# Turning the FFN's middle blocks in 32x32 pieces on VectorE and ScalarE instead of transposing them on TensorE

## The reference, cut to what matters

```python
def swiglu(h, wi, wo):
    g, u = jnp.split(h @ wi, 2, axis=-1)
    return (jax.nn.silu(g) * u) @ wo

def ffn_sublayer(x, shift, scale, gate, norm_w, wi, wo):
    return x + 0.5 * gate * swiglu(modulate(rms_norm(x, norm_w), shift, scale), wi, wo)
```

## Time and profile before

| | |
|---|---|
| time, median of 3 runs | 2223.12 us (2222.61 to 2223.47) |
| the profiled execution, from first to last instruction | 2220.9 us |
| TensorE busy | 2187.9 us, 99%, 10448 instructions |
| VectorE busy | 1634.8 us, 74% |
| ScalarE busy | 936.0 us, 42% |
| GpSimd busy | 64.5 us, 3% |
| share of the DMA queues, main one | 55.9% |

### The profile page before, as it was taken

The page is one execution under the profiler, slowest core; times in us unless marked ns, Lnnn a source line. Parts: engine busy times, 40 slices in busy tenths (PEclk is TensorE's granted clock), DMA queues, the critical chain, the costliest instruction groups (busy, mean ns, idle before and its releaser), DMA issues.

```text
span 2220.9 us, 28326 instructions
## 1 busy us (share of the span) xinstructions
PE 2187.9 (99%) x10448; PEld 1752.6 (79%) x10448; DVE 1634.8 (74%) x1881; ACT 936.0 (42%) x1098; POOL 64.5 (3%) x55
## 2 busy tenths in 40 slices
PE   6999999999999999999999999999999999999999
PEld 3568777777777778888888888888888888888887
DVE  3447888888888889756767888984577676776856
ACT  3333333333333346455554344464443444344443
POOL 0001000000000000001500000100000000000000
PEclk9999999999999999999999999999999999999999
DMA  9999888788888876555536776846665757567573
GB/s 364 387 369 307 286 315 314 270 293 290 306 301 283 281 262 222 198 171 170 186 114 228 269 254 233 278 159 207 228 227 190 264 189 264 189 195 259 188 228 132
DMA packets 273332, 548.13 MB, mean 247 GB/s; under 512 B 9014, under 2 KB 9418, under 8 KB 273008
## 3 DMA queue, kind: packets, MB, share of 16 engines
q1 hardware_dynamic: 212676, 423.69, 55.9%
q10 hardware_dynamic: 57484, 113.47, 14.2%
q0 software_dynamic: 3104, 10.05, 1.6%
HBM read 543.71 MB, written 3.46 MB: 246 GB/s over the span
## 4 chain that ended last, share of the span: by engine, by line
PE 94%; DVE 3%; DMA 1%; issue 1%; ACT 1%; SPq 0%; DVEq 0%; ACTq 0%
PE ps L697 29%; PE ps L699 29%; PE ps L698 29%; PE ps L638 1%; PE ps L623 1%; DMA ada_w_sb<-in_ada_w 1%; PE ps L774 1%; DVE w_lo L1789 1%; DVE acc L2003 0%; PE ps L1091 0%; PE ps L684 0%; PE ps L1159 0%; PE ps L1167 0%; DVE xm L1909 0%; ACT w_hi L1338 0%
## 5 line engine op out<-in xcount | busy, mean ns | idle before, releaser
L1338 ACT CAST w_hi<-raw_w 128x1024 fp32r<-128x1024 f32 x728 | 764.8, 1053 | 1162.2 <-PE ps L699 1114.1
L1789 DVE TENSOR_TENSOR w_lo<-raw_w,w_hi 128x1024 fp32r<-128x1024 f32 x728 | 896.5, 1235 | 405.3 <-ACT w_hi L1338 402.2
L697 PE MATMUL ps<-w_hi,xT_hi 128*128 128x512 f32 x2080 | 821.8, 395 | 5.6 <-DVE xT_lo L1877 4.2
L699 PE MATMUL ps<-w_hi,xT_lo 128*128 128x512 f32 x2080 | 811.1, 390 | 0.0
L698 PE MATMUL ps<-w_lo,xT_hi 128*128 128x512 f32 x2080 | 810.8, 390 | 0.0
L697 PEld LDWEIGHTS ps<-w_hi,xT_hi 128*128 128x128 f32 x2080 | 391.0, 188 | 110.2 <-issue 24.6
L699 PEld LDWEIGHTS ps<-w_hi,xT_lo 128*128 128x128 f32 x2080 | 391.0, 188 | 83.0
L698 PEld LDWEIGHTS ps<-w_lo,xT_hi 128*128 128x128 f32 x2080 | 391.3, 188 | 78.8
L1849 DVE SCALAR_TENSOR_TENSOR vec_acc<-ada_w_sb,ctile,vec_acc 128x512 f32<-128x512 f32 x420 | 299.0, 745 | 0.0
L697 PE MATMUL ps<-w_hi,hT_hi 128*128 128x512 f32 x704 | 276.4, 393 | 0.0
L699 PE MATMUL ps<-w_hi,hT_lo 128*128 128x512 f32 x704 | 274.3, 390 | 0.0
(11 more groups left out here) (277 smaller groups left out, 1037.8 us busy)
## 6 DMA issues: line engine op xcount, KB each, us to landing
raw_w<-in_ffn_wi SPq DMA_DIRECT2D x176, 1024.0 KB, 5.1
ada_w_sb<-in_ada_w ACTq DMA_DIRECT2D x96, 1024.0 KB, 8.3
raw_w<-in_ffn_wo SPq DMA_DIRECT2D x88, 1024.0 KB, 5.3
raw_w<-in_w_in SPq DMA_DIRECT2D x68, 1024.0 KB, 5.3
ada_w_sb<-in_ada_w SPq DMA_DIRECT2D x30, 1024.0 KB, 12.8
raw_w<-in_w_out SPq DMA_DIRECT2D x16, 1024.0 KB, 5.3
ada_m<-in_ada_w ACTq DMA_DIRECT2D x12, 1024.0 KB, 5.5
raw_w<-in_w_proj_m SPq DMA_DIRECT2D x8, 1024.0 KB, 5.3
```

Of the source, the lines that this page charges most:

```text
L697: pe.matmul(out, a_hi, w_hi[:, slot, kk, :], start=(first and kk == 0), stop=False)
L699: mm = pe.matmul(out, a_lo, w_hi[:, slot, kk, :], start=False, stop=(last and kk == 1))
L1338: act.copy(w_hi[:, us % SPL, :, :], raw_w[:, slot, 2 * half:2 * half + 2, :]).then_inc(hi_ready, 1)
L1789: dve.tensor_tensor(w_lo[:, us % SPL, :, :], raw_w[:, slot, 2 * half:2 * half + 2, :], w_hi[:, us % SPL, :, :].bitcast(F32), ALU.subtract) ...
```

## The change

19 of the 22 blocks are no longer transposed by TensorE. Block 0 of the first FFN and block 10 of both FFNs still are. For the others VectorE writes the product h with its 32-column pieces sorted anew (`h_product`), so that the piece b of each group of four lies in the quarter b of the row, and turns the whole row in 32x32 blocks in place. That leaves every block turned but in the wrong group of 32 partitions. `hT_move` carries them: for each of four source groups a of partitions ScalarE copies the four quarters b of the row to partition group b of `hT_raw`, which is the tile `sg` under another name, 16 copies of 32x256. They stand behind the weight casts of the units k = 2 to 5 of `ffn_out(i - 1)`, for block 0 of the second FFN behind those of `ffn_in(1)`, for block 1 of the first behind casts 37 to 40 of its opening. `hT_hi` and `hT_lo` are then made from `hT_raw`, at k = 2 of the next `ffn_in` where they were made at k = 0 (k = 6 in block 1 of the second FFN, there before at k = 2). Their layout has the token group outermost now, and `unit` reads it so. As `sg` is used until hT_lo is made, the next Silu waits for hT_lo. The second FFN's start on TensorE becomes a plain `ffn_in(1)`. Two semaphores, `h_turned` and `hT_moved`, are new.

The diff, without the same change of layout where hT_hi, hT_lo and hT2 are placed, and without the new semaphores' line:

```diff
@@ -287,6 +287,11 @@
         gate_dram = nc.dram_tensor("gate_dram", (3, KD, GROUPS, P), F32).ap()
         ident = cst[:, C_ID:C_ID + P]
+
+        h_flat = h[:].rearrange("p g c -> p (g c)")
+        h_parts = h_flat.rearrange("p (b x j) -> p x b j", b=4, j=32)
+        hT_raw = sg[:].rearrange("p g c -> p (g c)")
+        hT_raw_rows = hT_raw.rearrange("p (a x j) -> p x a j", a=4, j=32)
         raw_landed = sems("raw_landed", RAW)
@@ -363,6 +369,10 @@
                 return 16 * (c + 1)
             return 16 * (c + 1 - min(3, (c - 1) // 2 if c > 1 else 0)) if isinstance(c, int) else 16 * (c - 2)
+        def turned(f, i):
+
+            return i if f == 0 else FCH - 1 + i
+
         def at_least(eng, s, v):
             if not isinstance(v, int) or v > 0:
@@ -691,8 +701,8 @@
                 slot = us % SPL
                 for kk in halves:
                     for g in groups:
-                        a_hi = hi[:, kb + kk, g * P:(g + 1) * P]
-                        a_lo = lo[:, kb + kk, g * P:(g + 1) * P]
+                        a_hi = hi[:, kb + kk, g * P:(g + 1) * P] if len(hi.shape) == 3 else hi[:, g, kb + kk, :]
+                        a_lo = lo[:, kb + kk, g * P:(g + 1) * P] if len(lo.shape) == 3 else lo[:, g, kb + kk, :]
                         out = ps[:, banks + g, :]
                         pe.matmul(out, a_hi, w_hi[:, slot, kk, :], start=(first and kk == 0), stop=False)
                         pe.matmul(out, a_hi, w_lo[:, slot, kk, :], start=False, stop=False)
@@ -744,7 +754,7 @@
                     x_chunk(us, ux, 0, g_between, stage if first else None)
                     if not first:
                         pe.wait_ge(h_done, FCH * f + i)
-                        pe.wait_ge(acc_done, (ADDED + 4) * f + 4 * i - 3)
+                        at_least(pe, acc_done, (ADDED + 4) * f + 4 * i - 3)
                     x_chunk(us + 8, ux, 2, u_between)
                 def ffn_out(j, us, ux, between=None, mid=None):
@@ -771,8 +781,7 @@
                         pe.wait_ge(acc_done, (ADDED + 4) * f + 4 * i)
                     for b in range(4):
                         for g in range(GROUPS):
-                            mm = pe.transpose(ps[:, 4 + b // 2, (b % 2) * TOK + g * P:(b % 2) * TOK + (g + 1) * P],
-                                              h[:, g, b * P:(b + 1) * P], ident)
+                            mm = pe.transpose(ps[:, 4 + g, b * P:(b + 1) * P], h[:, g, b * P:(b + 1) * P], ident)
                     mm.then_inc(hT_ps, 1)
                 def prologue():
@@ -864,23 +873,13 @@
                     ada_q(ADA_PRE, 3)
                     whole(31)
                     ffn_out(0, u0 + 32, 0)
-                    h_transposes(1)
                 if f == 0:
                     prologue()
                 else:
                     ffn_in(0, u0, 0)
-                    pe.wait_ge(silu_done, FCH + 1)
-
-                    def g_between(k):
-                        if k == 1:
-                            h_transposes(0)
-
-                    x_chunk(u0 + 16, 0, 0, g_between)
-                    pe.wait_ge(h_done, FCH + 1)
-                    x_chunk(u0 + 24, 0, 2)
+                    ffn_in(1, u0 + 16, 0)
                     ffn_out(0, u0 + 32, 0)
-                    h_transposes(1)
                 def last():
                     i, e0 = FCH - 1, u0 + 32 + 24 * (FCH - 2)
                     hi, lo = (hT_hi, hT2_hi), (hT_lo, hT2_lo)
@@ -912,13 +911,7 @@
                 def step(i, between=None, mid=None):
                     ffn_in(i, u0 + 16, (i - 1) * 24, f == 0)
-
-                    def middle():
-                        if mid:
-                            mid()
-                        h_transposes(i)
-
-                    ffn_out(i - 1, u0 + 32, (i - 1) * 24, between=between, mid=middle)
+                    ffn_out(i - 1, u0 + 32, (i - 1) * 24, between=between, mid=mid)
                 if f == 0:
                     with pe.Fori(2, FCH - 1) as i:
@@ -1449,20 +1442,34 @@
             def ffn(f, u0):
                 def hT_hi_of(i):
-                    act.wait_ge(hT_ps, FCH * f + i + 1)
-                    act.copy(hT_hi[:].rearrange("p (a b) t -> p a (b t)", a=2), ps[:, 4:6, :]).then_inc(hT_hi_ready, 1)
+                    if f == 0 and isinstance(i, int) and i == 0:
+                        act.wait_ge(hT_ps, 1)
+                        act.copy(hT_hi[:].rearrange("p g k t -> p g (k t)"), ps[:, 4:6, :]).then_inc(hT_hi_ready, 1)
+                    else:
+                        act.wait_ge(hT_moved, 4 * turned(f, i))
+                        act.copy(hT_hi[:].rearrange("p g k (a j) -> p (g k) a j", a=4), hT_raw_rows).then_inc(hT_hi_ready, 1)
+
+                def hT_move(i, a):
+
+                    act.wait_ge(h_turned, turned(f, i))
+                    for b in range(4):
+                        ins = act.copy(hT_raw[32 * b:32 * b + 32, TOK * a:TOK * (a + 1)],
+                                       h_flat[32 * a:32 * a + 32, TOK * b:TOK * (b + 1)])
+                    ins.then_inc(hT_moved, 1)
                 def hT2_hi_of_last():
-                    act.wait_ge(hT_ps, FCH * (f + 1))
+                    act.wait_ge(hT_ps, 2 + f)
                     act.wait_ge(mac_done, VEC_Z if f == 0 else VEC_F2 + 4 * VEC)
-                    act.copy(hT2_hi[:].rearrange("p (a b) t -> p a (b t)", a=2), ps[:, 4:6, :]).then_inc(hT_hi_ready, 1)
+                    act.copy(hT2_hi[:].rearrange("p g k t -> p g (k t)"), ps[:, 4:6, :]).then_inc(hT_hi_ready, 1)
                 def ffn_in(i, us, ux, ada=False, last=False, g3=None):
                     first = isinstance(i, int) and i == 0
                     for k in range(16):
                         if not isinstance(i, int) or k or i:
                             split(us + k + AHEAD, ux)
-                        if not first and k == (2 if isinstance(i, int) and i == 1 else 0):
+                        if f == 1 and isinstance(i, int) and i == 1 and 2 <= k < 6:
+                            hT_move(0, k - 2)
+                        if not first and k == (6 if f == 1 and isinstance(i, int) and i == 1 else 2):
                             hT_hi_of(i - 1)
                         if g3 is not None and k == 0:
                             ada_vec(g3, [ada_w_sb[:, q, :, :] for q in range(4)], ada_landed, range(4), (g3 - 4 * G3) * VEC + VEC_F2)
@@ -1485,12 +1492,15 @@
                             act.wait_ge(units_done, us + ux + 8)
                             if not first:
                                 act.wait_ge(h_done, FCH * f + i)
+                                act.wait_ge(hT_lo_ready, FCH * f + i)
                             act.activation(sg[:], ps[:, 0:2, :], ACT.Silu).then_inc(silu_done, 1)
                 def step(i, ux, g3=None):
                     ffn_in(i, u0 + 16, ux, f == 0 and (not isinstance(i, int) or i > 1), False, g3)
                     for k in range(8):
                         split(u0 + 32 + k + AHEAD, ux)
+                        if 2 <= k < 6:
+                            hT_move(i, k - 2)
                         if f == 0:
                             if k == 5:
                                 ada_dve(i + 1, 1)
@@ -1519,6 +1529,8 @@
                         split(u0 + m, 0)
                         if m == 33:
                             hT_hi_of(0)
+                        if 37 <= m < 41:
+                            hT_move(1, m - 37)
                         if m == 35:
                             act.wait_ge(ada_used, 4 * VCH1)
                             for q in range(2):
@@ -1936,14 +1948,26 @@
             def ffn(f, u0):
                 def hT_lo_of(i):
                     dve.wait_ge(hT_hi_ready, FCH * f + i + 1)
-                    dve.tensor_tensor(hT_lo[:].rearrange("p (a b) t -> p a (b t)", a=2), ps[:, 4:6, :],
-                                      hT_hi[:].bitcast(F32).rearrange("p (a b) t -> p a (b t)", a=2),
-                                      ALU.subtract).then_inc(hT_lo_ready, 1)
+                    if f == 0 and isinstance(i, int) and i == 0:
+                        dve.tensor_tensor(hT_lo[:].rearrange("p g k t -> p g (k t)"), ps[:, 4:6, :],
+                                          hT_hi[:].bitcast(F32).rearrange("p g k t -> p g (k t)"),
+                                          ALU.subtract).then_inc(hT_lo_ready, 1)
+                    else:
+                        dve.tensor_tensor(hT_lo[:].rearrange("p g k (a j) -> p (g k) a j", a=4), hT_raw_rows,
+                                          hT_hi[:].bitcast(F32).rearrange("p g k (a j) -> p (g k) a j", a=4),
+                                          ALU.subtract).then_inc(hT_lo_ready, 1)
+
+                def h_product(i, u):
+
+                    dve.tensor_tensor(h_parts, sg[:].rearrange("p g (k b j) -> p (g k) b j", b=4, j=32),
+                                      u.rearrange("p g (k b j) -> p (g k) b j", b=4, j=32), ALU.mult).then_inc(h_done, 1)
```

(15 more changed lines are left out.)

9 lines of the change are left out of this document (5 added, 4 removed).

## The result

| | before | changed |
|---|---|---|
| median of 4 runs | 2222.86 us | 2203.38 us |
| lowest to highest | 2222.39 to 2223.47 | 2202.36 to 2203.78 |
| profiled span | 2220.9 us | 2201.7 us |

The ratio is 0.9911, 95% interval 0.9899 to 0.9923: 19.5 us, or 0.9%, faster. The forecast was 2203.0.

The account below looks back on a forecast made before the run. TensorE's instruction list was taken to bound the FFN stages; eleven blocks at 0.89 us and eight at 1.29 save 20.1, so 2220.9 - 20.1 + 2.2 = 2203.0 us. The eight-in-ten range was 2199 to 2211.

Parts of the forecast that it names:

- TensorE's list sets the FFN stages: Both FFNs: TensorE, 99% busy, sets their time; instructions taken off it shorten them if weights still arrive.
- 0.89 us for a plain block, 1.29 for one behind tiny matmuls: Savings on TensorE per removed block: eleven plain blocks, 9.8 us; eight of the first FFN (2 to 9), 10.3 us.
- The sum of 20.1: Both FFNs: total predicted saving of the 19 removed blocks, 20.1 us.
- what lies around the span: Outside the profiled span: 2.2 us, from the earlier median 2223.12 against the span 2220.9.
- Copy, turn, walks: ScalarE copy put at 421 ns, VectorE turn at 1244 ns, altered walks of h and hT_lo at nothing more.
- VectorE absorbs the turn in 11 us: First FFN behind h: a walk through VectorE's operations and idles absorbs the added 1.25 us within 11 us.
- 4.4 us at the next w_lo: VectorE behind the turn: w_lo ends at 456.3, TensorE wants it at 460.7, so 4.4 us to spare.
- ScalarE may fall 6.0 us behind: Weight casts in the FFNs: ScalarE can be 6.0 us late before TensorE stops.
- the VectorE rival: First FFN: VectorE or the fold for tiny matmuls takes over, giving 2213, or 2206 if only the wait returns; chance 0.10.
- the slower rival: Four units behind h: ScalarE's backlog 16c - 6.7 exceeds 6.0; gain gone at c = 0.86 us a copy; chance 0.03.
- its signs of being wrong: Copies over 0.75 us, doubled h or hT_lo with w_lo releasing TensorE, FFN clock below 1.00, or steps shrinking under 0.8 us.
- The first rival: First FFN gives part back: the turn's 1.25 us comes out of each of eight steps, 2213; chance 0.10.

Follow-up runs that it names:

- idle transposes: Changed kernel with eight identity transposes per turned block put back on TensorE, into an unread bank, without the wait for the addition to acc: 2219.5 us.
- both halves of the change: Two kernels made of the changed one, keeping the change only in the first FFN or only in the second: 2212.4 and 2214.5 us.
- turns5: Changed kernel with VectorE's turn of h made five times per block, each waiting for the one before: 2246.2 us.

## Why the prediction was right, step by step

- **TensorE's list sets the FFN stages.** Shown: eight idle transposes bring the second FFN's step back exactly, and both halves of the change shorten their own steps alone.
- **0.89 us for a plain block, 1.29 for one behind tiny matmuls.** Measured 0.91 and 1.28. The sum of 20.1 became 11.1 + 9.1 = 20.2 in the FFNs; the 1.04 us lost in the attention stage were not foreseen. That the total missed by 0.4 and not by 1.0 is partly luck: what lies around the span was put at 2.2 us and is 1.9 in the profiled run (2203.63 less 2201.7), and the median is 0.25 below that run.
- **Division of the 1.29.** Idle transposes put 0.81 to the transposes, 0.47 to the wait with its refill.
- **Copy, turn, walks.** 403 ns for 421, 1245 for 1244, nothing for the walks. A unit costs ScalarE 2.75 us where TensorE takes 2.72.
- **VectorE absorbs the turn in 11 us.** The walk came out row by row. But the spare time it gave, 4.4 us at the next w_lo (borne out by turns5 in the first FFN), is not the least there: between the end of the fold and its use are 1.7.
- **ScalarE may fall 6.0 us behind.** Near in the second FFN (5.7), wrong in the first (3.0, and with the lower clock that came with the waits a loss as if it were 1.5). The step that failed is the one from a cast to TensorE's use of that unit: it followed the weights and left out what VectorE does behind them in order. The number, 1.7 us between fold and tiny matmuls, stood in the earlier trace rows and was used for the VectorE rival alone. With it the slower rival's bound was mis-sized: as an estimate, with B for the backlog 16c - 6.7, eight blocks lose B - 3.0 and the others nothing while B is below 5.7, so the gain of 20 is used up at B = 5.5, which is c = (5.5 + 6.7) / 16 = 0.76 us a copy, not 0.86. If each of the eight lost the 1.6 us of the clock too, it would be 0.66. At the measured 0.41 B is about zero, so the forecast did not depend on it. No rival had the clock, which the prediction kept among its signs of being wrong.
- **The first rival** (VectorE passes its added time on in the first FFN) is true of the third turn on, not of the first.

## What to carry to other kernels

When one engine is 99% busy and the others wait for it, work that costs eight to nine times as much elsewhere (here 1.25 + 16 x 0.41 = 7.8 us for 0.91) can still be worth moving; price it by the gap it leaves between that engine's instructions, weight refills and waits included. Then spread the moved work so that no queue falls behind by more than its smallest lead: the same sixteen copies gave 0.9% faster behind four casts and 0.8% slower behind one, some 5 us of the latter through the clock, which fell behind the new waits. The smallest lead is found by following every result that the busy engine waits for, not the main stream alone, since an in-order queue hands its lateness to each small operation behind it.
